# Seven orders changed in a two-block DiT mixer kernel: opening, slab buffers, wkv ends and three attention starts

## What is computed

```python
def modulate(h, shift, scale):
    return h * (1.0 + scale) + shift

def swiglu(h, w_in, w_out):
    gate, up = jnp.split(h @ w_in, 2, axis=-1)
    return (jax.nn.silu(gate) * up) @ w_out
# every part: x = x + gate * part(modulate(rms_norm(x), shift, scale))
# block 1: FFN, even mixer (global grouped attention beside RWKV7), FFN,
#          FFN, odd mixer (window attention), FFN
# block 2: mixer of MLA attention beside mLSTM,
#          mixer of gated linear attention beside neighbourhood attention
# then a last rms_norm
```

## Time and profile before

| What | Value |
|---|---|
| time, median of 3 runs | 2582.37 us (2579.70 to 2583.63) |
| profiled execution, its own time | 2580.51 us |
| its span | 2577.6 us |
| TensorE busy | 2438.6 us, 95% |
| VectorE busy | 1679.6 us, 65% |
| ScalarE busy | 1055.6 us, 41% |
| GpSimd busy | 375.7 us, 15% |
| DMA, mean busy share of 16 engines | about 38% |

### The profile page before, as it was taken

How to read it: one execution, slowest core, us unless ns; L and a number is a source line. 1 busy time by engine, 2 the same in 40 slices (tenths; PEclk the granted TensorE clock), 3 DMA queues, 4 the chain that set the end, 5 groups by cost and what they waited for, 6 DMA issues and landing times.

```text
span 2577.6 us, 46166 instructions
## 1 busy us (share of the span) xinstructions
PE 2438.6 (95%) x17946; PEld 1984.0 (77%) x17946; DVE 1679.6 (65%) x2771; ACT 1055.6 (41%) x1744; POOL 375.7 (15%) x340
## 2 busy tenths in 40 slices
PE   6999999988898999999999999889999999899987
PEld 3888888857676788888788888679997875577866
DVE  2877787665555787788877754665555335665665
ACT  4222224365344622222522224455455244545354
POOL 2000001023253200000100001010013600121052
PEclk8999999999999999999999999999999999999999
DMA  6655663200000365566455542224562321013301
GB/s 248 243 190 194 194 205 116 89 22 3 4 4 21 120 208 192 194 196 203 164 195 190 192 136 94 93 72 158 180 179 99 98 86 50 1 66 125 127 19 50
DMA packets 88421, 323.34 MB, mean 125 GB/s; under 512 B 9712, under 2 KB 10864, under 8 KB 87504
## 3 DMA queue, kind: packets, MB, share of 16 engines
q1 hardware_dynamic: 86864, 310.68, 37.3%
q0 software_dynamic: 1408, 10.59, 1.1%
HBM read 320.18 MB, written 1.05 MB: 125 GB/s over the span
## 4 chain that ended last, share of the span: by engine, by line
PE 81%; DVE 9%; ACT 3%; issue 3%; DMA 1%; DVEq 1%; POOL 0%; POOLq 0%; ACTq 0%; SPq 0%
PE bank L502 22%; PE bank L503 22%; PE bank L504 22%; PE bank L1380 1%; DVE row_statistics L1434 1%; DVE weights_hi_lo L408 1%; DMA weight_ring<-stream_k 1%; PE bank L1389 1%; PE bank L2213 1%; ACT weights_hi_lo L403 1%; PE bank L1405 1%; PE bank L2219 1%; PE bank L1809 1%; PE bank L2849 1%; DVE work L3199 1%
## 5 line engine op out<-in xcount | busy, mean ns | idle before, releaser
L403 ACT ACTIVATE weights_hi_lo<-weight_ring 128x1024 fp32r<-128x1024 f32 (+1 forms) x381 | 396.6, 1042 | 1086.4 <-PE bank L504 1061.0
L408 DVE TENSOR_TENSOR weights_hi_lo<-weight_ring,weights_hi_lo 128x1024 fp32r<-128x1024 f32 (+1 forms) x374 | 455.2, 1217 | 480.7 <-ACT weights_hi_lo L403 479.1
L502 PE MATMUL bank<-input_hi,weights_hi_lo 128*128 128x512 f32 (+1 forms) x2032 | 743.5, 366 | 19.0 <-DVE input_lo L813 12.6
L503 PE MATMUL bank<-input_lo,weights_hi_lo 128*128 128x512 f32 (+1 forms) x2032 | 740.2, 364 | 0.0
L504 PE MATMUL bank<-input_hi,weights_hi_lo 128*128 128x512 f32 (+1 forms) x2032 | 740.0, 364 | 0.0
L502 PEld LDWEIGHTS bank<-input_hi,weights_hi_lo 128*128 128x128 f32 x2032 | 386.4, 190 | 85.9 <-issue 22.9
L503 PEld LDWEIGHTS bank<-input_lo,weights_hi_lo 128*128 128x128 f32 x2032 | 386.4, 190 | 59.8 <-issue 0.7
L504 PEld LDWEIGHTS bank<-input_hi,weights_hi_lo 128*128 128x128 f32 x2032 | 386.3, 190 | 59.9
L502 PE MATMUL bank<-hidden_hi_lo,weights_hi_lo 128*128 128x512 f32 (+1 forms) x952 | 342.8, 360 | 6.0 <-DVE weights_hi_lo L408 3.0
L503 PE MATMUL bank<-hidden_hi_lo,weights_hi_lo 128*128 128x512 f32 (+1 forms) x952 | 339.7, 357 | 0.0
L504 PE MATMUL bank<-hidden_hi_lo,weights_hi_lo 128*128 128x512 f32 (+1 forms) x952 | 339.7, 357 | 0.0
(11 more groups left out here) (524 smaller groups left out, 2946.6 us busy)
## 6 DMA issues: line engine op xcount, KB each, us to landing
weight_ring<-stream_k SPq DMA_DIRECT2D x498, 512.0 KB, 3.5
weight_ring<-stream_f SPq DMA_DIRECT2D x64, 448.0 KB, 3.4
weight_ring<-stream_f SPq DMA_DIRECT2D x32, 512.0 KB, 4.0
extra_tiles<-condrows POOLq DMA_DIRECT2D x3, 1024.0 KB, 8.9
constants<-consts POOLq DMA_DIRECT2D x1, 2112.5 KB, 9.2
residual_stream<-xin SPq DMA_DIRECT2D x1, 2048.0 KB, 11.6
work<-nabias POOLq DMA_DIRECT2D x1, 2048.0 KB, 9.5
residual_stream<-ctx POOLq DMA_DIRECT2D x1, 1024.0 KB, 5.9
```

Source lines behind the costliest of these rows:

```text
L403: act.activation(split_place(place)[:, 0, 0:words], w[:, 0:words], ACT.Copy).then_inc(hi_ready, 1)
L408: eng.tensor_tensor(split_place(place)[:, 1, 0:words], ring[:, n % RING, 0:words], split_place(place)[:, 0, 0:words].bitcast(F32), ALU.sub ...
L502: pe.matmul(out, weights[:, 0, w], x_hi, start=first, stop=False)
L503: pe.matmul(out, weights[:, 0, w], x_lo, start=False, stop=False)
```

## The change

- **Opening.** ScalarE splits slab 0, then modulates tile 0, splits slab 1, modulates tiles 1 to 4 and splits slab 2. VectorE makes the modulation first, and slab 1's and 2's low halves behind tiles 1 and 5.
- **First slab apart.** odd_out and l0_out, too, hold slab 0 in the `FIRST` buffer, and in all three output projections named the split of slab 2 waits for the stage before instead of slab 0.
- **wkv ends.** The outputs are added first and raise a semaphore of their own, for which ScalarE's copy waits; the two factors come behind. TensorE's products within a chunk run ahead of its wait for the factors.
- **Even attention.** The fifth head tile is normed with the other four, ahead of slab 20; the order of turns is 4, 0, 1, 2, 3; the attention's first turn runs between them, waiting for the norms alone.
- **MLA.** The scores of pair `it` wait for the first 2 (it + 1) heads' rotation, not for all eight; VectorE's first maxima come behind head 6.
- **Neighbourhood attention.** The scores of the first two pairs run ahead of the transposes of values and gated values; the gated values' copies go from VectorE to ScalarE, behind the first exponentials, and the third scores wait for them.

```diff
+FIRST_APART = ("odd_out", "l0_out", "l1_out")
-            return FIRST if stage == "l1_out" and k == 0 else EARLY if k == 2 else k
+            return FIRST if stage in FIRST_APART and k == 0 else EARLY if k == 2 else k
...
+        SPLITS_BEHIND = (0, 4)
@@ norm_scalar
                 first_mods_scalar(act, (3,))
-                for k in range(3):
-                    first_split_scalar(act, stage, k)
+                first_split_scalar(act, stage, 0)
...
                     ins.then_inc(modulated, 1)
+                if n == 0 and kt in SPLITS_BEHIND:
+                    first_split_scalar(act, stage, 1 + SPLITS_BEHIND.index(kt))
@@ norm_vector
             if n == 0:
-                first_splits_vector(dve, stage, (1,))
                 first_mods_vector(dve)
...
-                if n == 0 and kt == 1:
-                    first_splits_vector(dve, stage, (2,))
+                if n == 0 and kt - 1 in SPLITS_BEHIND:
+                    first_splits_vector(dve, stage, (1 + SPLITS_BEHIND.index(kt - 1),))
@@ residual_scalar
-                act.wait_ge(slab_done, p0 + m - 1)
+                act.wait_ge(slab_done, p0 + m - 1 if m > 2 or stage not in FIRST_APART else p0)
@@ residual_vector
-                split_lo(dve, 0, n0, s0 + 1)
+                split_lo(dve, first_place(stage, 0), n0, s0 + 1)
@@ attend_tensor
-            pe.wait_ge(heads_ready, a + 1)
-            pe.wait_ge(values_ready, a + 1)
+            if which == "odd":
+                pe.wait_ge(heads_ready, a + 1)
+                pe.wait_ge(values_ready, a + 1)
             if which == "mla":
+                pe.wait_ge(heads_ready, a + 1)
+                pe.wait_ge(values_ready, a + 1)
                 pe.wait_ge(rope_spread, 8)
-                pe.wait_ge(q_rotated, ODD_HEADS + 8)
+            if which == "na":
+                pe.wait_ge(heads_ready, a + 1)
             for it in range(n + 3):
+                if which == "even" and it == 0:
+                    pe.wait_ge(qk_normed, 5)
+                if which == "even" and it == 1:
+                    pe.wait_ge(max_ready, 1)
+                    pe.wait_ge(values_ready, 1)
+                if which == "even" and it == 2:
+                    pe.wait_ge(heads_ready, 1)
+                if which == "mla" and it < 4:
+                    pe.wait_ge(q_rotated, ODD_HEADS + 2 * it + 2)
+                if which == "na" and it == 2:
+                    pe.wait_ge(gv_ready, 1)
@@ even heads
-        EVEN_BANKS = (4, 5, 6, 7, 1)
+        EVEN_BANKS = (4, 5, 6, 7, 3)
+        EVEN_TURNS = (4, 0, 1, 2, 3)
...
-        def even_heads_tensor(pe):
-            even_sum(pe, 4)
-            for i in range(4):
+        def even_heads_tensor(pe, attention):
+            for i in EVEN_TURNS[:3]:
                 even_turn(pe, i)
             pe.wait_ge(*linear_copied(0, 20))
+            next(attention)
+            for i in EVEN_TURNS[3:]:
+                even_turn(pe, i)
...
-            even_turn(pe, 4)
...
-        def even_heads_vector(dve):
-            for i in range(4):
+        def even_heads_vector(dve, attention):
+            even_sine(dve, 4)
+            next(attention)
+            for i in EVEN_TURNS[1:]:
                 even_sine(dve, i)
             dve.drain()
-            for i in range(4):
+            for i in EVEN_TURNS:
                 even_rotated(dve, i)
-            even_norm(dve, 4)
...
             dve.drain().then_inc(heads_ready, 1)
@@ mla_heads_vector
+                if h == 6:
+                    next(attention)
@@ neighbourhood heads
-            turn_values(pe, BIG[:, 16:20, :], 4, 0).then_inc(values_turned, 1)
+            next(attention)
+            next(attention)
             pe.wait_ge(spans_used, 2)
+            turn_values(pe, BIG[:, 16:20, :], 4, 4).then_inc(values_turned, 1)
+            pe.wait_ge(values_ready, 4)
             turn_values(pe, BIG[:, 4:8, :], 4, 4).then_inc(gv_turned, 1)
...
-                ins = act.activation(WORK[:, 12 + tt, :], pb[tt][:, :], ACT.Copy)
+                ins = act.activation(WORK[:, 12 + tt, :], pb[4 + tt][:, :], ACT.Copy)
             ins.then_inc(values_ready, 1)
+            next(attention)
+            act.wait_ge(gv_turned, 1)
+            for tt in range(TT):
+                ins = act.activation(GVTOK[:, tt, :], pb[4 + tt][:, :], ACT.Copy)
+            ins.then_inc(gv_ready, 1)
...
-            dve.wait_ge(gv_turned, 1)
-            for tt in range(TT):
-                ins = dve.tensor_copy(GVTOK[:, tt, :], pb[4 + tt][:, :])
-            ins.then_inc(gv_ready, 1)
@@ wkv
+        outputs_added = sem("unit_outputs_added")
...
             if g:
-                pe.wait_ge(group_added, 2 * g - 1)
                 pe.wait_ge(inputs_copied, 2 * g - 1)
             if g == 2:
                 pe.wait_ge(state_ready, NCH)
             within(n0)
+            if g:
+                pe.wait_ge(group_added, 2 * g - 1)
...
-                    act.wait_ge(group_added, 2 * g + u + 1)
+                    act.wait_ge(outputs_added, 2 * g + u + 1)
...
-                dve.tensor_tensor(by_half(RR[:, j, :]), by_half(RR[:, j, :]), bank_pair(x, 0), ALU.add)
-                dve.tensor_tensor(by_half(EIT[:, j, :]), bank_pair(x, 1), on_cells(TAB("ident64")), ALU.add)
                 if d == 0:
                     ins = dve.tensor_copy(outputs, bank_pair(y, 0))
                 else:
                     ins = dve.tensor_tensor(outputs, outputs, bank_pair(y, 0), ALU.add)
-                ins.then_inc(group_added, 1)
+                ins.then_inc(outputs_added, 1)
+                dve.tensor_tensor(by_half(RR[:, j, :]), by_half(RR[:, j, :]), bank_pair(x, 0), ALU.add)
+                dve.tensor_tensor(by_half(EIT[:, j, :]), bank_pair(x, 1), on_cells(TAB("ident64")), ALU.add)\
+                   .then_inc(group_added, 1)
```

More of the change, by code:

```diff
@@ L1966, in wkv_ahead_vector @@
                 even_cosine(dve, i)
+            even_norm(dve, 4)
+            dve.drain()
+            even_cosine(dve, 4)
             yield
@@ L1999, in wkv_ahead_scalar @@
             even_square(act, 4)
-            for i in range(4):
+            for i in range(5):
                 even_root(act, i)
```

49 lines of the change are left out of this document (25 added, 24 removed).

## The result

The changed kernel takes 2564.92 us (median of 5 runs, 2560.08 to 2567.50), the kernel before 2579.70 in the same comparison (5 runs, 2576.93 to 2583.63): ratio 0.9935, 95% interval 0.9924 to 0.9946, that is 16.8 us less. The medians differ by 14.8. The profiled execution took 2560.08 us, 20.4 less than the one of before, where the prediction's sum was 13.5.

A forecast was written before the change was run, and what follows sets the result against it. TensorE, busy 95% of the span, bounds the kernel; savings are its idle and half-clock time. Terms 2.9 + 3.3 + 0 + 1.0 + 1.1 + 3.0 + 2.7 - 0.5 = 13.5 us gave median 2568.9, range 2563 to 2576.5.

The forecast's parts named there:

- Opening, 2.9: Kernel's start: modulation first brings the first product from 47.74 to 45.3, 2.4 us, plus 0.5 for the clock; bounds 2.0 to 4.1.
- The choice of L668's row over L813's own: Opening: VectorE's low-half operation is held by GpSimd's slab, as L668 was, so the gain is 2.4 us, not 3.4.
- The 0.5 added for a sooner rise of the clock: Opening: if the clock rises one or two us sooner behind the first product, half of that is saved.
- odd_out 3.3, l1_out 1.0, l0_out 0: Output projections: idle before slab 2 goes, 2.05 us plus 1.25 of half clock in odd_out, 1.0 in l1_out, none in l0_out.
- wkv 1.1: wkv ends: scan starts 0.7 us earlier, 0.2 at each of two group ends; bounds 0.5 to 2.0.
- Even 3.0: Even attention: third scores' maxima at 548.4 to 549.0 instead of 551.94, stage 3.0 us earlier; bounds 2.0 to 3.9.
- MLA 2.7: MLA: first scores fill the 3.17 us idle before the last rotation, gaining 2.7 us; lower bound 1.0.
- Neighbourhood attention, -0.5: Neighbourhood attention: VectorE sets the pace, third scores wait for ScalarE's copies; 0.5 us lost, bounds +0.2 to -2.9.
- the upper price: Rival, neighbourhood attention: transposes at half clock cost 2.9 us, 2.4 more than the sum, time 2571; chance 0.15.
- the one of fewer half-clock stretches: Rival: fewer half-clock stretches in even attention, scan and opening gain 0.9, 0.9 and 1.2 us more, time 2566; chance 0.08.
- early starts only move waits: Rival, attentions: the first pair's gain is waited for again at the fourth; 5.7 us lost, time 2574.6; chance 0.20.
- The clock staying low through the attentions: Rival, attentions: early scores break TensorE's work into shorter bursts, holding half clock; 2592 at 40 us of it; chance 0.02.

The follow-up runs named there:

- before_again: The kernel before, run again with no edit as a control; ratio 1.0004 to the kernel before.
- after_again: The changed kernel, run again with no edit; ratio 0.9934 to the kernel before, 17.0 us less.
- old start: Kernels without MLA's early scores; from ahead of MLA to behind mLSTM's second idle time 189.6 us (mean of 7).
- new start: Kernels with MLA's early scores; from ahead of MLA to behind mLSTM's second idle time 182.8 us (mean of 7).
- before_d: The kernel before with the 8 transposes of MLA's pair 10 done twice or three times; ratios 0.9993 and 0.9996.
- mla_d: The kernel before plus MLA's early scores, with pair 10's 8 transposes done twice or three times; ratios 0.9982 and 0.9983 to the kernel before.
- before_pad: The kernel before with TensorE's 8 transposes at mLSTM's start done three times, 1.4 us more work; ratio 0.9994.

## Why the prediction was right or wrong

The direction held, and every term but MLA's came within 0.8 us in the traces. The median, 2564.9, is inside the range; the profiled execution, 2560.1 with 20.4 us gained, is below it. The failing step is the price of the clock, in MLA's term. The sum held 2.7 us for MLA, all of it from the scores' earlier start, and nothing for the half clock at its scores or behind them. It measured 6.8 in the traces and 8.0 (4.6 to 11.1) in its own run. The sum charged an idle time at most with the half-clock stretch right behind it, 1.75 us in all, and took all stretches elsewhere as fixed. Behind the first product the first pair of profiles shows 9.1 us for the clock, the second (before_again, after_again) 4.9; the gain of 17 less the 9 to 10 of idle time leaves about 7.

- **Opening, 2.9.** Measured 2.3 in its run, and 2.4 from ScalarE's first split to the first product, as forecast without the clock. With the slab landing 1.36 us earlier the forecast 45.3 becomes 43.94; it was 43.95. The choice of L668's row over L813's own was right: L815 took 1.78 us here and 2.20 in after_again, beside a GpSimd slab. The Trainium skill's "SBUF — State Buffer", section "Who interferes with whom", says that a VectorE instruction with two inputs in SBUF contends with a GpSimd instruction that reads SBUF, and the trace agrees: the half of L815 that met the slab took 1.38 us instead of 0.47. The 0.5 added for a sooner rise of the clock was wrong: 5.35 us behind the first product, as before.
- **odd_out 3.3, l1_out 1.0, l0_out 0.** 3.8, 1.2 and none in the traces, 5.4 (3.1 to 7.7) in the run.
- **wkv 1.1.** 1.35 in the trace up to the first scan and 1.0 behind the second; 0.5 in its run, which cannot tell it from 0.
- **Even 3.0.** 2.6 in the traces; the third maxima came 9.25 us behind slab 20, not 8.2 to 8.7. I gave the rotations 0.42 us each; one of the five took 1.50 beside GpSimd's L2422. It is the contention that I had priced in the opening. The kernel before paid for it as well, at L1590, so the edit did not bring it in but moved it.
- **MLA 2.7.** At its own place 3.2 against the first profile of before and 4.3 against the mean of the seven with the old start and no delay, since with the new start the scores run at full clock. Behind it, at idle times that the change does not touch, two stretches of half clock of 1.6 us each can go, since they depend on how far the idle time lies behind the last stretch ahead of it: the first always, the second in 4 of 7. The before_d and mla_d kernels show this. That makes 4.3 + 1.6 + 0.9 = 6.8; the rest of the 8.0 is inside the interval.
- **Neighbourhood attention, -0.5.** -0.7 in the first profile, and in the second the upper price: transposes of 2.89 us, third scores 11.1 us behind the first; -0.8 on average. The runs, 1.0 us of gain alone and 0.5 to 0.8 within the change, don't tell it from -0.5 in their intervals.
- With the means of the traces the sum is 2.4 + 3.8 + 1.2 + 1.1 + 2.6 + 6.8 - 0.8 = 17.1 us; measured 16.8, interval 13.9 to 19.6.
- The upper bounds that the prediction gives add to 14.6 us without MLA, which has none; 17.9 comes out with the 3.3 by which its third maxima were to come earlier. So even all upper bounds together missed the 6.8 of this part.

Of the rivals, the one of fewer half-clock stretches (0.08) was the nearest: it named the right cause, but at other places. In the even attention, the scan and the opening, which it named, the stretches were shorter or as long as before, and none was gone. That early starts only move waits failed, though third scores do still wait 1.9 to 2.1 us, which I had named as what would speak against me. The clock staying low through the attentions did not come: PEclk is 1.00 in MLA's start.

What stays open: why the distance behind the last stretch decides, and so whether a kernel could be arranged to dodge all stretches. Open too is what shortened the stretch at 1746 in the changed kernel's first profile; it was shorter in before_again as well, where nothing was edited.

## What to carry to other kernels

Split a gain into TensorE's idle and busy time before believing a sum. If busy time changed for the same products, look whether half of the busy time in half-clock stretches changed by as much; if so, the clock gave it, and one profile of each kernel is not enough. Compare one place over many profiles, by the time between the same two products: here that repeats to 0.1 us where no clock step falls (odd_out, MLA's new start), while whole executions differ by several us. An edit that moves work by a microsecond can add or remove half-clock stretches far behind it, so price a moved stage with an uncertainty of some 1.6 us for each later idle time of 1 to 2 us. When VectorE's two-input operations are moved, look at what GpSimd does at the new place, at every one of them.

## What the runs showed of the hardware that I had not expected

- The same idle time (1.02 us at mLSTM's start, 2.04 later) was followed by half clock or not according to its distance from the last half-clock stretch: delays of 1.03 and 2.06 us of work ahead switched the two stretches off and on separately, and in undelayed kernels 505.19 us went with half clock and 505.27 without.
- A half-clock stretch does not need an idle time of 1 us right ahead of it: in before_pad it came with that time filled by 64 x 64 transposes.
- Added work can be free: with 1 to 2 us of repeated transposes the kernel before took from 0.5 us less to 0.4 more at that place (0.9993 and 0.9996 of the whole time), and the new start of MLA 2.6 to 2.9 us more.
- The first product starts anywhere between 41.98 and 48.37 us, and ScalarE's first split, which waits for a transfer, between 33.99 and 40.31, a spread as large as the gain of several of these parts. From the one to the other it is 7.98 to 8.23 us.
- Total idle time seemed to repeat (139.0 and 138.8; 128.7 and 130.0), but in part by luck. In the kernel before, behind the first product it was 116.7 and 118.8 us, and busy time there 2413.2 and 2412.9. In the changed kernel it was 110.2 and 112.2, and busy time 2404.2 and 2408.0. One profile of each kernel gives either to some 2 to 4 us.
